# Moving the second factors, sigmoids, decay sums and removal norms of a recurrent mixer into its projection

## The reference, cut to what matters

```python
z = jnp.einsum('btd,de->bte', h, P['w_in_even'][li])          # z_rwkv: its last 1792 columns
...
zz = z + (shifted - z) * P['rwkv_mu'][li]
r, k, v, zw, za, zg = jnp.split(zz, offs, axis=-1)            # 512, 512, 512, 64, 64, 128
w_log = -jax.nn.softplus(-(P['rwkv_w0'][li] + jnp.tanh(zw) @ P['rwkv_w2'][li])) - 0.5
decay = jnp.exp(-jnp.exp(w_log))
a = jax.nn.sigmoid(P['rwkv_a0'][li] + za @ P['rwkv_a2'][li])
g = jax.nn.sigmoid(zg) @ P['rwkv_g2'][li]
kk = hd(k * P['rwkv_kk'][li])
kk = kk * lax.rsqrt(jnp.maximum(jnp.sum(kk * kk, axis=-1, keepdims=True), 1e-24))
k_mod = hd(k * (1.0 + (a - 1.0) * P['rwkv_ka'][li]))
# then: y, s_t = scan over tokens with r, decay, k_mod, v, kk, a
```

## Time and profile before

| What | Value |
|---|---|
| Median of 3 runs | 1896.12 us (1892.9 to 1901.09) |
| Profiled execution | 1892.59 us, span 1890.8 us, mean granted clock 0.954 |
| PE busy | 1770.0 us (94% of the span) |
| DVE / ACT / POOL busy | 836.6 / 525.2 / 696.1 us |
| Projection block on PE | 416.27 to 508.17 us |
| Preparation block | 513.06 to 574.27 us |

### The profile page before, as it was taken

How to read it: one execution, slowest core, us unless ns; L and a number is a source line. 1 busy time by engine, 2 the same in 40 slices (tenths; PEclk the granted TensorE clock), 3 DMA queues, 4 the chain that set the end, 5 groups by cost and what they waited for, 6 DMA issues and landing times. The chain is left out here.

```text
span 1890.8 us, 36210 instructions
## 1 busy us (share of the span) xinstructions
PE 1770.0 (94%) x15772; PEld 1690.7 (89%) x15772; DVE 836.6 (44%) x1654; ACT 525.2 (28%) x896; POOL 696.1 (37%) x278
## 2 busy tenths in 40 slices
PE   6989798779768999899999999999999999999997
PEld 6987688569745998799999999999999999999997
DVE  4251586225573444465430355444235555024531
ACT  5132454322241222232221222331223222112221
POOL 1300000012202111355653555655655655445641
PEclk8988699989978999899999999999999999999999
DMA  5540420513200100122222222322222222222222
GB/s 146 122 57 23 148 90 13 162 48 94 60 1 22 37 4 28 46 89 90 68 73 85 88 90 65 92 91 90 68 89 90 68 90 73 84 90 90 66 78 76
DMA packets 158379, 140.90 MB, mean 75 GB/s; under 512 B 16178, under 2 KB 153942, under 8 KB 157838
## 3 DMA queue, kind: packets, MB, share of 16 engines
q1 hardware_dynamic: 158222, 138.60, 24.8%
HBM read 132.68 MB, written 10.02 MB: 75 GB/s over the span
## 5 line engine op out<-in xcount | busy, mean ns | idle before, releaser
L270 POOL TENSOR_TENSOR w_lo<-w_raw,w_hi 128x2048 fp32r<-128x2048 f32 (+3 forms) x109 | 459.3, 4214 | 783.9 <-ACT w_hi L264 783.7
L309 PE MATMUL ps<-h_hi,w_hi 128*128 128x288 f32 x2016 | 434.1, 296 | 0.0
L309 PE MATMUL ps<-h_hi,w_lo 128*128 128x288 f32 x2016 | 433.4, 296 | 0.0
L309 PE MATMUL ps<-h_lo,w_hi 128*128 128x288 f32 x2016 | 433.2, 296 | 0.0
L264 ACT ACTIVATE w_hi<-w_raw 128x2048 fp32r<-128x2048 f32 (+3 forms) x109 | 190.1, 1744 | 501.9 <-PE ps L309 458.5
L309 PEld LDWEIGHTS ps<-h_hi,w_hi 128*128 128x128 f32 x2016 | 324.0, 189 | 0.3
L309 PEld LDWEIGHTS ps<-h_hi,w_lo 128*128 128x128 f32 x2016 | 323.7, 189 | 0.0
L309 PEld LDWEIGHTS ps<-h_lo,w_hi 128*128 128x128 f32 x2016 | 323.5, 189 | 0.0
L418 DVE TENSOR_TENSOR xT<-ps,xT 128x576 f32<-128x576 f32 x48 | 35.6, 756 | 264.7 <-PE ps L309 264.7
L309 PE MATMUL ps<-g_lo,w_hi 128*128 128x288 f32 x704 | 151.1, 295 | 0.0
L309 PE MATMUL ps<-g_hi,w_lo 128*128 128x288 f32 x704 | 151.0, 295 | 0.0
(11 more groups left out here) (497 smaller groups left out, 2794.5 us busy)
## 6 DMA issues: line engine op xcount, KB each, us to landing
w_raw<-in_ffn_up SPq DMA_DIRECT2D x44, 1024.0 KB, 5.0
w_raw<-in_ffn_down SPq DMA_DIRECT2D x16, 768.0 KB, 4.8
w_raw<-in_w_in_odd SPq DMA_DIRECT2D x12, 1024.0 KB, 5.1
w_raw<-in_ffn_down SPq DMA_DIRECT2D x16, 640.0 KB, 4.4
w_raw<-in_w_in_even SPq DMA_DIRECT2D x7, 1024.0 KB, 5.4
w_raw<-in_w_in_even SPq DMA_DIRECT2D x6, 872.0 KB, 9.6
BT<-rv SPq DMA_DIRECT2D x8, 520.0 KB, 3.6
seg<-in_cache_cmp_kv SPq DMA_DIRECT2D x32, 128.0 KB
```

The costliest lines, as they stand in the source:

```text
L270: pool.tensor_tensor(slab_view(wlo[slot], st), slab_view(raw[slot], st), slab_view(whi[slot], st).bitcast(F32), ALU.subtract).then_inc(w_l ...
L309: last = pe.matmul(ps[:, bank + 2 * j + half, 0:HT], w[slot][:, c:c + 128], x[:, xs + t, half * HT:(half + 1) * HT], start=(t == 0 and n = ...
```

## The change

The projection goes through its slabs in another order, `RW_ORDER`: the one with tiles 12 and 13 (zw, za, zg) first, then k, r and v. Its loops are unrolled. A tile now has a bank pair of its own, three pairs (0-1, 2-3, 4-5) in turn; banks 6 and 7 are for the second factors and the sums of squares. ACT evacuates a tile at a time. Between the tiles of the projection, in each engine's program, stands work that was in the preparation block: after tiles 3 to 10 one of the eight second-factor products on PE and, one tile later, its sigmoid on ACT; the squares on ACT; the decay sums on DVE; after tile 12 the sums of squares on PE; at the end the bound, root and reciprocal. The preparation block keeps four DMAs, the spreading back, `scaled` and the transposes.

The core of the diff:

```diff
+        RW_ORDER = (6, 2, 3, 0, 1, 4, 5)
+        st_rw = stage(7, KT, 256, lambda s: cols(w_in, 0, KT, W_NSA + 256 * RW_ORDER[s], 256))
...
 SP, projection block
+                    sp.dma_start(lora2[0:64, :], a["rwkv_w2"][0]).then_inc(k2_in, 16)
+                    sp.dma_start(lora2[64:128, :], a["rwkv_a2"][0]).then_inc(k2_in, 16)
+                    sp.dma_start(keep_seq[:, :], k["keep"]).then_inc(k2_in, 16)
+                    sp.dma_start(hsum_k[:, :, :], k["headsum"]).then_inc(k2_in, 16)
...
 ACT, projection block
+                    def evacuate(i):
+                        n, j, kk = i // 2, i % 2, tile_of(i)
+                        if j == 0:
+                            act.wait_ge(first_done, n + 1)
+                        else:
+                            act.wait_ge(slab_done, st_rw["base"] + n + 1)
+                        act.wait_ge(rx_used, i + 1)
...
+                        if j == 1:
+                            act.wait_ge(rx_ready, i + 1)
+                            act.nop().then_inc(banks_free[n % 2], 1)
+                    def sigmoids(n):
+                        c = n // 2
+                        act.wait_ge(wa_ps, n + 1)
+                        out, bias = (decay_in[c][:, :], V_W0 + c) if n % 2 == 0 else (rate[c], V_A0 + c)
+                        act.activation(halves(out), ps[:, 6:8, 0:HT], ACT.Sigmoid, bias=vec[:, bias:bias + 1]).then_inc(sig_ready, 1)
...
+                    for i in range(14):
+                        if i % 2 == 0:
+                            split_hi(act, *follow(st_rw["base"] + i // 2 + 1))
+                        evacuate(i)
...
+                        if 4 <= i < 12:
+                            sigmoids(i - 4)
+                        if 8 <= i < 12:
+                            square(i - 8)
+                    act.wait_ge(ss_m, 1)
+                    act.activation(knorm, knorm, ACT.Sqrt).then_inc(ss_std, 1)
...
 PE, projection block
+                    def tile(i):
+                        n, j, b = i // 2, i % 2, 2 * (i % 3)
+                        g = st_rw["base"] + n
+                        if j == 0:
+                            pe.wait_ge(w_lo_ready, g + 1)
+                        if i >= 3:
+                            pe.wait_ge(rx_ready, i - 2)
...
+                    def second_factor(n):
+                        c, part = n // 2, slice(64 * (n % 2), 64 * (n % 2) + 64)
+                        if n == 0:
+                            pe.wait_ge(k2_in, 64)
+                            pe.wait_ge(act_lora, 1)
+                            pe.wait_ge(sh_ev, 1)
+                        else:
+                            pe.wait_ge(sig_ready, n)
+                        for half in range(2):
+                            last = pe.matmul(ps[:, 6 + half, 0:HT], lora2[part, 128 * c:128 * c + 128], zz[part, 12, half * HT:(half + 1) * HT], start=True, stop=True)
+                        last.then_inc(wa_ps, 1)
+                    for i in range(14):
+                        tile(i)
+                        if 3 <= i < 11:
+                            second_factor(i - 3)
+                        if i == 12:
+                            pe.wait_ge(sig_ready, 8)
+                            pe.wait_ge(sq2_ready, 4)
+                            for c in range(4):
+                                for half in range(2):
+                                    last = pe.matmul(ps[0:NH, 6 + half, 0:HT], hsum_k[:, c, :], k_squares[c][:, half * HT:(half + 1) * HT], start=(c == 0), stop=(c == 3))
+                            last.then_inc(ss_ps, 1)
...
 DVE, projection block
+                    for i in range(14):
+                        tile(i)
+                        if i == 4:
+                            dve.wait_ge(k2_in, 64)
+                        if i in (5, 7, 9, 11):
+                            decay_sums((i - 5) // 2)
+                    dve.wait_ge(ss_ps, 1)
+                    dve.tensor_scalar(halves(knorm), ps[0:NH, 6:8, 0:HT], 1e-24, None, ALU.max).then_inc(ss_m, 1)
+                    dve.wait_ge(ss_std, 1)
+                    dve.reciprocal(knorm, knorm).then_inc(nrm_ready, 1)
...
 preparation block: SP, then ACT
-                    sp.dma_start(w2[0:64, :], a["rwkv_w2"][0]).then_inc(k_in, 16)
-                    sp.dma_start(w2[64:128, :], a["rwkv_a2"][0]).then_inc(k_in, 16)
-                    sp.dma_start(keep[:, :], k["keep"]).then_inc(k_in, 16)
...
                     for c in range(4):
                         act.wait_ge(cm_ready, c + 1)
+                        act.activation(PI[c][:, :], decay_sum[c], ACT.Exp, scale=-1.0)
+                        act.activation(tt_[c][:, :], decay_sum[c], ACT.Exp)
+                        act.activation(sg[c][:, :], decay_in[c][:, :], ACT.Exp).then_inc(exp_ready, 1)
```

More of the change, by code:

```diff
@@ L1895, in even_mixer @@
             ext = [r.take("z_ext", [128, 1 + TP + NB * (TS + 1)]) for _ in range(2)]
-            df = [r.take("z_diff", [128, TP + NB * (TS + 1)]) for _ in range(2)]
+            df = r.take("z_diff", [128, TP + NB * (TS + 1)])
             sh_rows = r.take("sh_rows", [NB * RT, 128])
+            decay_in = [r.take("log_decay_in", [128, T]) for _ in range(4)]
+            decay_sum = [mixf[:, 4 + c, :] for c in range(4)]
+            rate = [zz[:, ROW_B + c, :] for c in range(4)]
+            k_squares = [zz[:, ROW_A + c, :] for c in range(4)]
+            keep_seq = r.take("keep_seq", [128, T])
+            lora2 = r.take("lora2", [128, 512])
+            hsum_k = r.take("headsum_k", [128, 4, NH])
+            knorm = zz[0:NH, ROW_A, :]
             slots_at = nc.sbuf_base + (-nc.sbuf_base) % 64
@@ L1950, in _ @@
+                    act.wait_ge(ss_m, 1)
+                    act.activation(knorm, knorm, ACT.Sqrt).then_inc(ss_std, 1)
                 @block.gpsimd
                 def _(pool):
-                    with pool.Fori(0, 3) as i:
-                        split_lo(pool, st_rw, i, 1, 2)
-                        split_lo(pool, st_rw, i, 2, 2)
-                    split_lo(pool, *follow(st_rw["base"] + 7))
+                    for n in range(1, 8):
+                        split_lo(pool, *follow(st_rw["base"] + n))
@@ new lines, in tile @@
+                    def tile(i):
[5 more added lines that the diff above has]
+                            pe.wait_ge(rx_ready, i - 2)
+                        for t in range(KT):
+                            c = 256 * t + 128 * j
+                            for m, (w, x) in enumerate(((whi, hhi), (whi, hlo), (wlo, hhi))):
+                                for half in range(2):
+                                    last = pe.matmul(ps[:, b + half, 0:HT], w[g % 2][:, c:c + 128], x[:, t, half * HT:(half + 1) * HT],
+                                                     start=(t == 0 and m == 0), stop=(t == KT - 1 and m == 2))
+                        if j == 0:
+                            last.then_inc(first_done, 1)
+                        else:
+                            last.then_inc(slab_done, 1)
@@ L1998, in even_mixer @@
             r = Region(R)
-            sg, aa, kk_, tt_ = ([r.take(x, [128, T]) for _ in range(4)] for x in ("log_decay", "rate", "removal", "decay"))
-            keep = r.take("keep", [128, T])
+            sg, PI, kk_, tt_ = ([r.take(x, [128, T]) for _ in range(4)] for x in ("decay_before", "decay_inv", "removal", "decay"))
+            omk = r.take("rate_scaled", [128, T])
             hones = r.take("headones", [128, 128])
@@ L2081, in _ @@
-                    pe.wait_ge(act_lora, 1)
-                    for c in range(4):
-                        if c >= 2:
-                            pe.wait_ge(sig_ready, c - 1)
-                        b = wa_bank(c)
-                        for half in range(2):
-                            cols_ = slice(half * HT, (half + 1) * HT)
-                            pe.matmul(ps[:, b + half, 0:HT], w2[0:64, 128 * c:128 * c + 128], zz[0:64, 12, cols_], start=True, stop=True)
-                            last = pe.matmul(ps[:, b + 2 + half, 0:HT], w2[64:128, 128 * c:128 * c + 128], zz[64:128, 12, cols_], start=True, stop=True)
-                        last.then_inc(wa_ps, 1)
@@ L2091, in _ @@
-                    pe.wait_ge(sig_ready, 4)
-                    for c in range(4):
-                        pe.wait_ge(sq2_ready, c + 1)
-                        for half in range(2):
-                            last = pe.matmul(ps[0:NH, half, 0:HT], hsum[:, c, :], squares_[c][:, half * HT:(half + 1) * HT], start=(c == 0), stop=(c == 3))
-                    last.then_inc(ss_ps, 1)
+                    pe.wait_ge(k_in, 64)
                     pe.wait_ge(nrm_ready, 1)
```

154 lines of the change are left out of this document (53 added, 101 removed).

## The result

The changed kernel takes 1907.85 us (median of 11 runs, 1896.63 to 1924.03) where the kernel before takes 1895.81 us (11 runs, 1884.05 to 1901.74). The ratio is 1.0068 with an interval of 1.0042 to 1.0095: slower by 12.0 us between the medians. (A ratio with an interval is the one on record, against the runs of the kernel before that are recorded with it; it is not the quotient of two medians.) The profiled execution took 1907.85 us, with a span of 1906.1 us; it is 15.3 us longer than that of before. Runs of one kernel scatter with the clock: of the 29 runs of the kernel before that are on record with the first four experiments, the fastest took 1881.76 us at a mean granted clock of 0.963 and the slowest 1907.58 us at 0.947, so a profiled execution is compared here by its stretches and not by its whole time.

The account below looks back on a forecast made before the run. PE was taken to bound the projection and to wait in the preparation block: +24.9 us projection, -18.3 behind it, +6.2 clock falls make +12.8, 1905.4 on the profiled execution or 1908.9 on the median; forecast 1907 us, range 1898 to 1920.

Parts of the forecast that it names:

- Second factors: In the projection on PE: eight products of four records at 0.24 us, standing alone between tiles, add 8.45 us.
- Sums of squares: In the projection on PE: 16 records, two groups of 8 started 1.93 us apart, add 3.87 us.
- Seven stops: Behind tiles 4 to 10 PE waits for ACT's copies and sigmoid, 1.72 or 1.9 us each, 12.6 us.
- Clock falls: In the projection: four of seven stops lower PE's clock, 1.55 us each, 6.2 us; one to seven falls: chance 0.64.
- New order, bank pairs: Rest of the projection: slabs ready, DMAs early enough, bank pairs three tiles old when reused; costs nothing.
- Projection: The projection on PE grows 24.9 us at full clock; some 116 us long, 122 with four falls, from 92.
- End to spreading back: From the projection's end to the spreading back: 12.2 us where it was 30.56, gaining 18.3 us.
- Sum: Whole kernel: +6.6 us at full clock plus 6.2 for the clock, +12.8 us; forecast 1907 us.
- The cover: In the projection, 18 us between slabs hide ACT's rounding and DVE's decay sums; if gone, four sums cost 10 us.
- That the clock holds: Rival, projection: stops bring no clock fall, so +6.6 us, 1899 on the profiled execution, 1903 on the median; chance 0.21.
- that it stays low: Rival, projection: clock low from first stop to last, seven tiles longer by 30 us, 1929 us; chance 0.09.
- That the stops are covered: Rival, projection: sigmoids done when PE asks, growth 12.3 us alone, net -6.0, 1887 to 1890 us; chance 0.06.

Follow-up runs that it names:

- the first four experiments: Changed kernel with, separately: sigmoids ahead of copies (1887.51 us), matmuls filling the stops (1900.27), idle copies lengthening them (1921.15), norms before the last tile (1903.47).
- The paired step: Changed kernel with sigmoids ahead of copies, and each second-factor step taking decay and rate together for half the tokens: 1880.75 us, 0.9930 of before.
- the first experiment: Changed kernel with ACT's sigmoids and squares put ahead of a tile's copies, PE's order untouched: 1887.51 us, 0.9972 of before.
- the norms moved: Changed kernel with bound, root and reciprocal taken ahead of tile 13 on DVE and ACT: 1903.47 us, 1.0039 of before.
- the early table: Changed kernel with the spreading-back table loaded during the projection, PE waiting for the other tables behind the spreading back: 1906.18 us, one run.
- lengthening: Changed kernel with two unread copies on ACT ahead of each of seven sigmoids: 1921.15 us (4 runs), 1.0158 of before.
- the filled kernel: Changed kernel with 12 unread matmuls on PE before each of the seven waits for a sigmoid: 1900.27 us, 1.0040 of before.
- the kernel with all three edits: Changed kernel with sigmoids first and paired second factors, norms ahead of the last tile, and spreading-back table loaded early: 1877.54 us, 0.9904 of before.

## Why the prediction was right

The forecast was 1907 us and slower; 1907.85 was measured. Step by step, with what the profiled executions showed:

| Term | Forecast | Measured |
|---|---|---|
| Second factors | 8.45 | 8 x 1.35 = 10.8 |
| Sums of squares | 3.87 | 534.39 - 530.32 + 0.10 = 4.17 |
| Seven stops | 12.6 | 4 x 1.66 + 3 x 1.88 = 12.3 |
| Clock falls | 4 x 1.55 = 6.2 | 4 x 1.52 = 6.1 |
| New order, bank pairs | 0 | 0 |
| Low stretch at the projection's head | not counted | 0.44 x (4.99 - 4.61) = 0.2 |
| Projection | +31.1 | +33.6 (terms: 33.6) |
| End to spreading back | -18.3 | -19.1 |
| Sum | +12.8 | +15.3 with the rest of the span |

**The work** was the term most off, by 2.7 us, and it is nearly all that the projection's sum lacks (2.5 us). The step took 0.24 us a record right; a second factor still has four records 0.24 us apart. What it left out is the change from one kind of matmul to the other: PE starts a second factor 0.22 us after the last matmul of a tile instead of 0.133, the next tile 1.16 us after it, not 4 x 0.24 = 0.96, and that tile's second matmul 0.24 us after its first and not 0.133: 0.39 us a step. The paired step pays the same (0.88 us for 2 x 0.24), so it is paid for each step and not for each record. The Trainium skill's page "TensorEngine Tiling (Array Packing)", section "Key Properties", says that a change of the tiling mode drains TensorE first; the 0.39 us a step agree with that in kind, but no run here separates a drain from other causes.

**The stops** came where and for the reason that was given, 1.66 and 1.88 us for 1.72 and 1.9, and the first experiment shows the reason: with the sigmoid ahead of the copies all seven are gone.

**The falls.** Four were forecast and four came, but that number is partly luck: the kernels with the norms moved and with the early table have the same seven stops and fell six times (23.9 us at the lower level) and five times (20.5 us). 0.44 of that time is what the projection loses: theirs took 130.44 and 128.41 us, 23.75 and 21.72 more than the one without stops (106.69), and 12.3 us of stops with 10.6 and 9.1 of clock, and 0.8 and 0.2 for the low stretch at the head, make 23.7 and 21.6. The price of one fall, 1.55 us, was read right. That the idle time brings them is shown from both sides, by filling and by lengthening. The length of a single stop does not decide: in the change one of the four stops of 1.59 us was followed by a fall and all three of 1.81, with the norms moved all four of 1.59 and two of the three of 1.81. What picks one and not the next stays open. The Trainium skill's page "TensorE: Matmul & The Clock Gate", section "A second HAM failure mode: psum-queue depth-cycling", which the forecast took to mean seven falls, is right in kind: with PE's brief idling between groups the clock swings here. In number the traces lie between, at four to six of seven, and the filled kernel and the one with the sigmoid ahead cycle through the same banks without one, so that here it is the idling and not the cycling.

**Behind the projection** the chain was as forecast, and the spreading back was released by a table load. It is 0.7 us shorter since the four loads were issued within 1.26 us and not 1.6, and the last landed 1.88 us after its issue and not 2.36. The 0.53 us for an issue was a mean over seven loads of 0.41 to 0.64; the last four of them already stood 0.41 to 0.48 apart. From the spreading back to the last copy of the token rows it took 35.5 us (552.55 to 588.09), as said. The cover held: PE waited for no slab, and the decay sums delayed nothing.

**The rivals.** That the clock holds and that it stays low are both refuted by the four stretches. That the stops are covered did not happen in this change, for the order on ACT, which the forecast named as the condition. Made true in the first experiment, it gave 1887.5 us, within the 1887 to 1890 worked out for it (about 1891 by its ratio), though the work cost 2.7 us more than that sum had it. The profiled executions differ by 2.5 us more than the forecast's sum, and its 1907 lay between two bases; the closeness to 1907.85 is better than the terms. The lengths that it gave for the projection, some 116 us and 122 with four falls, are short of its own terms by one (91.9 + 24.9 = 116.8, and 123.0); 125.5 was measured.

## What to carry to other kernels

Work moved into a stretch where an engine has no idle time is paid there in full, and a wait moved with it is paid a second time through the clock; so before moving it, look at what stands ahead of the releasing instruction on the other engine, and put that instruction first where its input is ready. Here one such reordering turned a loss of 12 us into a gain of 5 to 9, and pairing the half-row products and shortening the chain behind it made it some 18. Products on half of the rows cost less when they are moved in pairs on both halves: 0.88 us for four records here, and 1.35 one by one.

## What the runs showed of the hardware

Adding matmuls made a projection shorter: 84 that nothing reads, 10.5 us of PE's time laid into stops of unchanged length, took away all four falls, and the projection went from 125.50 to 119.83 us.

A fall to half the clock did not double the time of a matmul: those of 288 columns start 0.133 us apart at 1.0 and 0.24 at 0.5. With 0.44 of the low time as its price the projections of all these kernels come out to 0.2 us.

Small products with short stops between them did not hold the clock: with 0.83 us of waiting at each, the granted clock went to 0.50 and PE took 2.28 us for what had taken 1.23.

A scan on DVE that starts just behind the forming of a low part on POOL is held until that has ended, as the timeline of the kernel with all three edits shows:

```profile
501.08 4.67 POOL L271 TENSOR_TENSOR w_lo<-w_raw,w_hi 128x2048 fp32r<-128x2048 f32 x1 [9.86 <-ACT w_hi L265]
501.36 5.61 DVE L2076 TENSOR_TENSOR_SCAN mixf<-keep_seq,log_decay_in 128x576 f32<-128x576 f32 x1
```

It ended 1.22 us after POOL's instruction (501.36 + 5.61 against 501.08 + 4.67); in the kernel with the work behind the projection, where POOL does nothing beside it, the same scan takes 1.36 us. All twelve scans that began so, 0.28 to 0.36 us behind POOL's, took 5.6 us (four in each kernel with the sigmoid ahead). In the change the scans began 0.2 to 1.0 us ahead of POOL's instruction and took 1.36; there the difference behind them, another operation on two tiles, took 4.9 us and not 0.75. The scaling on one tile took its 0.45 us beside POOL as well. None of this cost time here, since DVE had it to spare.
